# A two-network kernel: where weights are split, where x is scaled, and how the first keys take their turns

## The chip, the cores and the metric

The kernel runs on one core of a Trainium2 chip. The metric is the device time of one execution in microseconds (us). The engines are TensorE (PE in the rows; PEld is its weight load), VectorE (DVE), ScalarE (ACT), GpSimd (POOL) and SyncE (SP), which issues most of the DMAs. Each engine works through its own queue in order; semaphores order the queues among each other.

## The reference, cut to what matters

Two networks run one after the other on x of 512 tokens by 1024 channels. The first has two layers, each an attention mixer and a convolutional gated feed-forward net, and a last norm:

```python
for layer in range(2):
    h = rmsnorm(x, attn_norm[layer])
    x = x + (even_mixer(h, ...) if layer == 0 else odd_mixer(h, ...))
    x = x + conv_glu_ffn(rmsnorm(x, ffn_norm[layer]), ...)
return rmsnorm(x, final_norm)
```

The even mixer holds a stick-breaking attention of 8 heads and a sparse attention of 8 heads; the odd mixer is a forgetting attention of 16 heads. The second network takes that x and a context of 256 tokens:

```python
h  = modulate(rmsnorm_2(x, norm1_g), sh1, sc1);  hc = modulate(rmsnorm_2(ctx, norm1_g), sh1_c, sc1_c)
y_a = neighborhood_attention(q, k, v, k_c, v_c, rpb);  y_b = spatial_gating(gu, gv, ...)
x = x + g1 * merge_branches(y_a, y_b, ga, gb, ...)
x = x + g2 * peer_ffn(modulate(rmsnorm_2(x, norm2_g), sh2, sc2), wq, keys, u, v)
return rmsnorm_2(x, final_g)
```

The first network's last norm scales x itself, since the second network adds to the scaled x. In `peer_ffn` 16 query blocks of 128 columns are scored against 128 keys each, and the 16 best of each are taken.

## The kernel before, in words

**Units.** All weights come in units of 128 output columns by 1024 inputs (some by 1408). SyncE fetches each unit into one of four raw buffers (`fetch_weights`, L182). Products have close to fp32 precision by splitting: ACT rounds the raw unit to `w_hi` (`split_hi`, L201, the copy is L207), and DVE (`split_lo`, L209, L213) or POOL (`split_lo_pool`, L215, L220) makes `w_lo`, what is left. There are two buffers of each, taken in turn, so `split_hi(u)` waits until unit u - 2 has been used. A unit is 24 matmuls of PE on `h_hi` and `h_lo` (`unit`, L222, L239): 16 with `w_hi`, then 8 with `w_lo`. It is a generator that stops after every third matmul, so a block is three matmuls, and `run(steps, n)` issues n blocks. With `ready` it waits for h part by part (eight parts k, one for each 128 channels).

**Norms.** A norm adds squares on POOL, sums them on PE, takes the root on ACT and DVE, spreads it with PE over a bank, and then makes the eight h parts (`shifted_vector`, L408): DVE scales (L413), ACT rounds to `h_hi` (L406), DVE leaves `h_lo` (L416). `norm` (L418) is this for `norm2`, whose h feeds the keys.

**Twin norm.** `twin_norm` (L514) takes the last norm of the first network and the first norm of the second together. While ACT and DVE make the h parts for the neighbourhood attention, POOL scales x in place, two operations for each of eight parts (L576, L578). `ended` and `after` (L278, L282) close a stage: `after(engine, name)` lets an engine wait for all that the named stage has put on PE, DVE, ACT and POOL. The neighbourhood attention (`neighbour`, L1689) begins on ACT, DVE and POOL with such an `after` on the twin norm. There `first_tensor` alternates five blocks of the key unit and five of the value unit, then ends both, then runs the query unit. Sixteen steps follow, four for each of four pairs of heads, with the next pair's units laid between the steps. POOL makes the masks `na_less` of each pair (L1925), three operations each.

**Stacked attentions.** `stick` (stick-breaking, four pairs of heads) and `fox` (forgetting, eight pairs) take four steps for each pair (i = 0 to 3). Pair p + 1's three units (key, query, value) run in blocks between the steps of pair p. What ACT and DVE must do for them is written in two generators, `stacked_scalar` (L1268) and `stacked_vector` (L1281), which the step loop takes up twice in each step with `run(more, 1)`: once behind the first half of the step, once behind the second half. In `stick`, DVE's first half of step m makes `sb_z` and `sb_low` of m (L1454, L1459), and its second half makes the scan and sum of step m - 1 (L1468, L1472). On ACT, the first half ends with Ln and, at i = 0, with the values' copy (L655), and the second half is the exponential of step m - 1 (L1429), which PE turns (L1376) one step later. In `fox` the second half is the exponential (L1600) and the normalisation of step m itself (L671).

**Keys.** `keys` (L2176) runs 16 units on `norm2`'s h. Behind each, ACT copies the query (L2207), PE scores it against the keys (L2194), ACT copies the scores (L2214), and DVE picks the best 16. POOL splits all `w_lo` from the second unit on.

Of the kernel before, what the change touches and what calls it, by code (L numbers as in the profile page):

```python
# [12 lines left out]
ALU = mybir.AluOpType  # L13
# [103 lines left out]
def program(nc, io, table):  # L117
# [38 lines left out]
    def col(name, k=0, n=1):  # L156
        return cols[:, COLS[name] + k:COLS[name] + k + n]
# [258 lines left out]
                ve.scalar_tensor_tensor(lo[:, k - 1, :], hf[(k - 1) % 2][:, 0:n], shift(k - 1), hi[:, k - 1, :], ALU.add, ALU.subtract).then_inc(*dve.next("h", name, k - 1))  # L416

    def norm(name, before, squares, gain, shift):  # L418
        def tensor():
            after(te, before)  # L420
            sums_tensor(name, squares)
            spread_tensor(name, hf[0], t_bank[1])

        def scalar():
            after(sc, before)
            sc.preload_act_table_set("sqrt_and_others")
            root_scalar(name, stat[:, 8:12], stat[:, 4:8])
            for k in range(KT):
                shifted_scalar(name, k, h_hi, T, shift)

        def vector():
            after(ve, before)
            rstd_vector(name)
            ve.wait_ge(*pe.at(name, "spread"))
            shifted_vector(name, x, t_bank[1][:, :], h_hi, h_lo, T, gain, shift)

        tensor()
        scalar()
        vector()
        ended(name)  # L440
# [73 lines left out]
    def twin_norm(name, ctx_name, before, squares, U, hc_blocks):  # L514
# [53 lines left out]
            ve.wait_ge(*pe.at(name, "spread"))  # L568
            shifted_vector(name, x, t_bank[1][:, :], h_hi, h_lo, T, gain, shift)

        def gpsimd():

            gp.wait_ge(*act.at("final", "rstd"))
            for k in range(KT):
                gp.wait_ge(*dve.at(name, "scaled", k))
                gp.tensor_scalar(x[:, k, :], x[:, k, :], col("final_norm", k), None, ALU.mult).then_inc(*pool.next())  # L576
                gp.wait_ge(*pool.here())
                gp.tensor_tensor(x[:, k, :], x[:, k, :], ny[:, :], ALU.mult).then_inc(*pool.next("final x", k))  # L578

        tensor()  # L580
        scalar()
        vector()
        gpsimd()
        ended(ctx_name)

# [678 lines left out]
        return te.matmul(out, q[:, hh, tile], k_lo[:, hh, keys], start=False, stop=True)  # L1266

    def stacked_scalar(U, B, name, p):  # L1268
        yield
        split_hi(U[0] + 1)  # L1270
        yield
        yield
        split_hi(U[1] + 1)
        key_hi(B, name, p)
        yield
        yield
        split_hi(U[2] + 1)
        query_hi(B, name, p)
        yield

    def stacked_vector(U, B, name, p, gain=None, flip=False):  # L1281
        q, k_hi, k_lo, qf, kf, v, vT = B
        yield
        split_lo(U[0] + 1)
        yield
        ve.wait_ge(*w_used.at(U[0]))
        if p:
            ve.wait_ge(*pe.at(name, "v turned", p - 1))
        scaled(kf[:, ::-1] if flip else kf[:, :], lin[U[0] % 2][:, :]).then_inc(*dve.next(name, "k", p))
        bank_of.taken(U[0], dve)  # L1290
        yield
        split_lo(U[1] + 1)
        yield
        key_lo(B, name, p)
        yield
        ve.wait_ge(*w_used.at(U[1]))
        if gain is None:
            scaled(qf[:, :], lin[U[1] % 2][:, :]).then_inc(*dve.next(name, "q", p))
        else:
            ve.scalar_tensor_tensor(qf[:, :], lin[U[1] % 2][:, :], gain, ny[:, :], ALU.mult, ALU.mult).then_inc(*dve.next(name, "q", p))  # L1300
        bank_of.taken(U[1], dve)
        yield
        query_lo(B, name, p)
        yield
        split_lo(U[2] + 1)
        ve.wait_ge(*w_used.at(U[2]))
        scaled(vT[:, ::-1] if flip else vT[:, :], lin[U[2] % 2][:, :]).then_inc(*dve.next(name, "v", p))
# [381 lines left out]
    def neighbour(norm_name, before, st, y_hi, y_lo, U, hc_blocks):  # L1689
# [222 lines left out]
        def gpsimd():  # L1912
            after(gp, before)
            for edge in (slice(0, NA_EDGE), slice(NA_EDGE + T, NA_CTX)):
                for t in (k[0], k[1], vT):
                    gp.memset(t[:, edge], 0.0).then_inc(*pool.next("na edges"))
            for s in range(2):
                gp.memset(less[s][:, 6, :], 0.0).then_inc(*pool.next())
            gp.wait_ge(*mask_in.at("in"))
            for p in range(4):  # L1920
                gp.wait_ge(*bias_in[p % 2].at(p))
                if p >= 2:
                    gp.wait_ge(*dve.at("na least", 1, 4 * (p - 1) - 1))
                for edge in range(3):
                    gp.tensor_tensor(less[p % 2][:, 2 * edge:2 * edge + 2, :], mask[:, edge, :].unsqueeze(1).to_broadcast([P, 2, NA_BAND]), bias[p % 2][:, :, :],  # L1925
                                     ALU.subtract).then_inc(*pool.next("na less", p))
# [249 lines left out]
    def keys(before, st, vals, index, work):  # L2176
# [4 lines left out]
        keys_in = loaded("keys_in")  # L2181

        def tensor():
            for j in range(17):
                if j < 16:
                    run(h_unit(U[j], (lambda k: dve.at("h", before, k)) if j == 0 else None))
                if j:
                    b = (j - 1) % 2
                    te.wait_ge(*act.at("query", j - 1))
# [7 lines left out]
        def scalar():  # L2197
            after(sc, before)
            sc.dma_start(keysT[:, :, :], io["keys"]).then_inc(*keys_in.next("in"))
            for j in range(17):  # L2200
                if j < 16:
                    u = U[j]
                    split_hi(u + 1)
                    sc.wait_ge(*w_used.at(u))
                    if j >= 2:
                        sc.wait_ge(*pe.at("key scores", j - 2))
# [19 lines left out]

        def gpsimd():
            after(gp, before)
            gp.wait_ge(*w_lo_made.at(U[0]))
            for u in U:  # L2230
                split_lo_pool(u + 1)

        tensor()
# [824 lines left out]
```

## Time and profile before

| | us |
|---|---|
| median of 3 runs | 3115.46 (3110.76 to 3118.15) |
| the profiled execution, its own time | 3110.99 |
| its span, first to last instruction | 3109.5 |
| TensorE matmul busy in the span | 2990.8 (96%) |
| VectorE busy | 2261.2 (73%) |
| ScalarE busy | 1337.1 (43%) |
| GpSimd busy | 803.2 (26%) |

The mean granted TensorE clock of the profiled execution is 0.986 of full speed. Busy shares are averages over stages with different limits; times of the stages are read in the trace, in us from the start of the span. In it the stick attention's steps run from 223, those of the forgetting attention from 770, the twin norm's h parts from 1379, the neighbourhood attention's scores from 1420, and the keys from 1799.

### The profile page before, as it was taken

The numbers are of one execution on the slowest core, as the hardware profiler recorded it, in microseconds if no ns is written. First come the engines' busy times: TensorE is split into PE (matmuls) and PEld (weight loads), VectorE is DVE, ScalarE is ACT, GpSimd is POOL, SyncE is SP. The second block draws the span as 40 slices with busy tenths as digits, with TensorE's granted clock in tenths as the row PEclk, the third lists the DMA queues.
The fourth block names the chain that finished last, engine by engine and source line by source line (L and its number), as shares of the span: only waits on it lengthen the run. The fifth ranks groups of instructions, "written<-read, shape, count | busy, mean of one in ns | idle before, by whom it ended". The sixth has DMA issues, their size and how long they took to land. (4 is left out here: it accounts for less than half of the span.)

```text
span 3109.5 us, 43156 instructions
## 1 busy us (share of the span) xinstructions
PE 2990.8 (96%) x16088; PEld 2603.5 (84%) x16088; DVE 2261.2 (73%) x4398; ACT 1337.1 (43%) x2346; POOL 803.2 (26%) x696
## 2 busy tenths in 40 slices
PE   7998899999999999998999989999999999999998
PEld 5666688887777888876778779999999999999998
DVE  4768586775885877743453468978788888988886
ACT  3667532233664323333442234348843333444333
POOL 1000100001001200042000124668744445434431
PEclk9999999999999999999999989999999999999999
DMA  4001244433222444321123223656699999999993
GB/s 149 27 31 49 85 153 143 133 108 105 90 87 96 161 139 132 108 69 57 45 78 102 91 79 111 197 175 231 236 365 330 324 346 337 342 332 321 338 339 117
DMA packets 189710, 525.33 MB, mean 169 GB/s; under 512 B 15792, under 2 KB 80176, under 8 KB 187200
## 3 DMA queue, kind: packets, MB, share of 16 engines
q1 hardware_dynamic: 130432, 308.84, 29.2%
q0 software_dynamic: 45104, 164.68, 14.9%
q10 hardware_dynamic: 13968, 49.06, 4.1%
q8 instruction: 129, 2.11, 0.3%
q14 instruction: 77, 0.63, 0.1%
HBM read 484.22 MB, written 38.31 MB: 168 GB/s over the span
## 5 line engine op out<-in xcount | busy, mean ns | idle before, releaser
L239 PE MATMUL bank<-h_hi,w_hi 128*128 128x512 f32 (+1 forms) x2528 | 958.4, 379 | 44.6 <-DVE h_lo L325 13.1
L239 PE MATMUL bank<-h_lo,w_hi 128*128 128x512 f32 (+1 forms) x2528 | 941.8, 373 | 0.0
L213 DVE TENSOR_TENSOR w_lo<-w_raw,w_hi 128x1024 fp32r<-128x1024 f32 (+1 forms) x452 | 580.2, 1284 | 274.3 <-ACT w_hi L207 255.5
L207 ACT ACTIVATE w_hi<-w_raw 128x1024 fp32r<-128x1024 f32 (+1 forms) x508 | 544.8, 1073 | 458.8 <-PE bank L239 437.4
L239 PE MATMUL bank<-h_hi,w_lo 128*128 128x512 f32 (+1 forms) x2528 | 590.9, 371 | 0.1
L239 PEld LDWEIGHTS bank<-h_hi,w_hi 128*128 128x128 f32 x2528 | 480.2, 190 | 125.7 <-issue 25.6
L239 PEld LDWEIGHTS bank<-h_lo,w_hi 128*128 128x128 f32 x2528 | 481.5, 190 | 58.0 <-issue 2.2
L239 PEld LDWEIGHTS bank<-h_hi,w_lo 128*128 128x128 f32 x2528 | 459.2, 189 | 61.8 <-issue 4.6
L239 PE MATMUL bank<-e_hi,w_hi 128*128 128x384 f32 x1024 | 345.8, 338 | 2.3 <-DVE x L2711 2.0
L239 PE MATMUL bank<-e_lo,w_hi 128*128 128x384 f32 x1024 | 344.5, 336 | 0.0
L2532 POOL DMA_INDIRECT own_row<-in_u_rows,own_e x128 | 166.2, 1298 | 259.7 <-DVE sums L2667 206.6
L2532 POOL DMA_INDIRECT own_row<-in_v_rows,own_e x128 | 176.4, 1378 | 205.5 <-DVE own_row L2661 164.9
L239 PE MATMUL bank<-e_hi,w_lo 128*128 128x384 f32 x1024 | 198.3, 336 | 0.0
L239 PEld LDWEIGHTS bank<-e_hi,w_hi 128*128 128x128 f32 x1024 | 192.5, 188 | 5.8 <-ACT w_hi L207 2.4
L239 PEld LDWEIGHTS bank<-e_lo,w_hi 128*128 128x128 f32 x1024 | 192.7, 188 | 0.0
L239 PEld LDWEIGHTS bank<-e_hi,w_lo 128*128 128x128 f32 x1024 | 179.4, 188 | 0.0
L220 POOL TENSOR_TENSOR w_lo<-w_raw,w_hi 128x1024 fp32r<-128x1024 f32 x56 | 139.2, 2489 | 140.6 <-ACT w_hi L207 140.5
L333 POOL MEMSET sums<- 128x512 f32 x6 | 3.2, 530 | 635.7 <-DVE o_lo L1476 315.2
L2667 DVE SCALAR_TENSOR_TENSOR sums<-own_row,acc_c,sums 128x1024 f32<-128x1024 f32 x127 | 162.5, 1280 | 3.8 <-DVE sums L2667 0.5
L2661 DVE SCALAR_TENSOR_TENSOR own_row<-own_row,own_h 128x1024 f32<-128x1024 f32 x128 | 153.3, 1218 | 0.0
L1054 POOL DMA_DIRECT2D ada_w<-in_ada_w x48 | 25.7, 536 | 467.1 <-DVE ada_w L1073 455.6
L2505 POOL TENSOR_SCALAR oneB<-iota,jT 128x128 f32<-128x128 f32 x192 | 140.5, 748 | 20.2 <-PE bank L2439 16.6
(442 smaller groups left out, 4443.6 us busy)
## 6 DMA issues: line engine op xcount, KB each, us to landing
w_raw<-in_w SPq DMA_DIRECT2D x476, 512.0 KB, 3.9
ada_w<-in_ada_w POOLq DMA_DIRECT2D x48, 512.0 KB, 3.6
expert_weights<-G ACTq DMA_DIRECT2D x12, 2048.0 KB, 7.1
Gin<-expert_weights SPq DMA_DIRECT2D x32, 768.0 KB, 10.1
w_raw<-in_w SPq DMA_DIRECT2D x32, 704.0 KB, 4.0
hidden_ahead<-u_stage ACTq DMA_DIRECT2D x56, 192.0 KB, 3.9
ahead<-hidden_ahead SPq DMA_DIRECT2D x28, 384.0 KB, 8.4
fx_crow<-fox_cum POOLq DMA_DIRECT2D x8, 512.0 KB, 4.0
```

What stands on the lines that cost most here:

```text
L207: sc.activation(w_hi[s][:, 0:n], w_raw[raw_slot[u]][:, 0:n], ACT.Copy).then_inc(*w_hi_made.next(u))
L213: ve.tensor_tensor(w_lo[s][:, 0:n], w_raw[raw_slot[u]][:, 0:n], w_hi[s][:, 0:n], ALU.subtract).then_inc(*w_lo_made.next(u))
L220: gp.tensor_tensor(w_lo[s][:, 0:n], w_raw[raw_slot[u]][:, 0:n], w_hi[s][:, 0:n], ALU.subtract).then_inc(*w_lo_made.next(u))
L239: m = te.matmul(out, wt, moving, start=(not low and k == 0 and moving is hi), stop=(low and k == len(blocks) - 1))
L333: gp.memset(acc[:, :], 0.0).then_inc(*pool.next())
L1054: gp.dma_start(w[r][:, :], io["ada_w"][n]).then_inc(*tile_in[r].next(n))
L2505: gp.tensor_scalar(B[s % HOLD][:, n, :], iota[:, :], jT[:, t:t + 1], None, ALU.is_equal).then_inc(*pool.next("one B", s))
L2532: gp.indirect_dma_start(ring[n % RING][:, :], None, io["u_rows" if kind == "u" else "v_rows"], bass.IndirectOffsetOnAxis(ap=own_e[:, slot: ...
L2661: ve.scalar_tensor_tensor(row, row, 1.0, own_h[:, :, :], ALU.mult, ALU.mult, accum_out=own_a[:, slot:slot + 1]).then_inc(*dve.next("own ro ...
L2667: ve.scalar_tensor_tensor(own_y, row, own_w[:, slot:slot + 1], own_y, ALU.mult, ALU.add).then_inc(*dve.next("own row", n))
```

## The change

- `stacked_scalar` and `stacked_vector`: the split of the pair's second unit stands ahead of the generator's first stop, no longer behind it. This applies to both attentions.
- `norm`: ACT and DVE split the unit behind the next one (the keys' second), ACT ahead of its `after`, DVE behind it and ahead of the root.
- `twin_norm`: POOL's scaling of x is taken out, and `neighbour` calls it on POOL behind the masks of its second pair.
- `keys`: the first two units alternate in five blocks each, both waiting for h part by part. ACT leaves out its first split, and POOL begins with the third unit.

```diff
     def norm(name, before, squares, gain, shift):
+        nxt = taken_units[0]
...
         def scalar():
+            split_hi(nxt + 1)
             after(sc, before)
...
         def vector():
             after(ve, before)
+            split_lo(nxt + 1)
             rstd_vector(name)
...
-        def gpsimd():
-
-            gp.wait_ge(*act.at("final", "rstd"))
-            for k in range(KT):
-                ...
...
-        gpsimd()
         ended(ctx_name)
+
+    def final_x_pool(name):
+
+        gp.wait_ge(*act.at("final", "rstd"))
+        for k in range(KT):
+            gp.wait_ge(*dve.at(name, "scaled", k))
+            gp.tensor_scalar(x[:, k, :], x[:, k, :], col("final_norm", k), None, ALU.mult).then_inc(*pool.next())
+            gp.wait_ge(*pool.here())
+            gp.tensor_tensor(x[:, k, :], x[:, k, :], ny[:, :], ALU.mult).then_inc(*pool.next("final x", k))
...
     def stacked_scalar(U, B, name, p):
+        split_hi(U[0] + 1)
         yield
-        split_hi(U[0] + 1)
         yield
...
         q, k_hi, k_lo, qf, kf, v, vT = B
+        split_lo(U[0] + 1)
         yield
-        split_lo(U[0] + 1)
         yield
...
             for p in range(4):
+                if p == 2:
+                    final_x_pool(norm_name)
                 gp.wait_ge(*bias_in[p % 2].at(p))
...
         def tensor():
+            firsts = [h_unit(u, lambda k: dve.at("h", before, k)) for u in U[:2]]
+            for _ in range(5):
+                run(firsts[0], 1)
+                run(firsts[1], 1)
             for j in range(17):
                 if j < 16:
-                    run(h_unit(U[j], (lambda k: dve.at("h", before, k)) if j == 0 else None))
+                    run(firsts[j] if j < 2 else h_unit(U[j]))
...
-                    split_hi(u + 1)
+                    if j:
+                        split_hi(u + 1)
...
-            gp.wait_ge(*w_lo_made.at(U[0]))
-            for u in U:
+            gp.wait_ge(*w_lo_made.at(U[1]))
+            for u in U[1:]:
                 split_lo_pool(u + 1)
```

## Rows read from the trace of the kernel before

**Rows 1.** Groups by line: shapes, count | busy us, mean ns | idle before, releasers.

```profile
L239 PE MATMUL bank<-h_hi,w_hi 128*128 128x512 f32 (+1 forms) x2528 | 958.4, 379 | 44.6 <-DVE h_lo L325 13.1 <-ACT na_k L1754 10.3 <-DVE h_lo L416 9.1
```

**Rows 2.** Timeline, twin norm into neighbourhood attention: start, length, engine, operation [idle, releaser].

```profile
1381.16 0.75 DVE L416 SCALAR_TENSOR_TENSOR h_lo<-norm_h,mod,h_hi 128x512 fp32r<-128x512 f32 x1 [0.72 <-ACT h_hi L406]
...
1392.36 1.76 DVE L416 SCALAR_TENSOR_TENSOR h_lo<-norm_h,mod,h_hi 128x512 fp32r<-128x512 f32 x1
...
1394.18 0.74 PE L239 MATMUL bank<-h_hi,w_hi 128*128 128x512 f32 x2 [1.16 <-DVE h_lo L416]
...
1397.49 1.98 PE L239 MATMUL bank<-h_hi,w_lo 128*128 128x512 f32 x8
...
1404.35 1.26 POOL L578 TENSOR_TENSOR x<-x,norm_y 128x512 f32<-128x512 f32 x1
...
1408.06 1.06 ACT L207 ACTIVATE w_hi<-w_raw 128x1024 fp32r<-128x1024 f32 x1
...
1409.74 0.76 PE L239 MATMUL bank<-h_hi,w_hi 128*128 128x512 f32 x1 [10.28 <-ACT na_k L1754]
1409.79 5.64 POOL L1925 TENSOR_TENSOR na_less<-na_mask,na_bias 128x512 f32<-128x512 f32 x3 [2.81 <-DMA na_bias<-in_bias]
...
1416.05 1.98 PE L239 MATMUL bank<-h_hi,w_lo 128*128 128x512 f32 x8
1417.87 0.92 PE L651 MATMUL bank<-ident,na_vT 128*128 128x128 f32 x7
...
1419.59 0.71 PE L1817 MATMUL bank<-na_k,na_q 64*128 64x256 f32 x4 [0.80 <-ACT na_v L655]
```

**Rows 3.** Timeline of `norm2` and the first keys.

```profile
1789.32 1.26 POOL L337 TENSOR_TENSOR sums<-sums,norm_h 128x512 f32<-128x512 f32 x1 [4.31 <-ACT norm_h L330]
...
1792.87 0.16 DVE L385 TENSOR_SCALAR stat<-bank 128x4 f32<-128x4 f32 x1 [4.29 <-PE bank L346]
...
1798.49 0.75 DVE L416 SCALAR_TENSOR_TENSOR h_lo<-norm_h,mod,h_hi 128x512 fp32r<-128x512 f32 x1
...
1807.17 1.62 DVE L416 SCALAR_TENSOR_TENSOR h_lo<-norm_h,mod,h_hi 128x512 fp32r<-128x512 f32 x2
...
1808.88 0.33 ACTq L2199 DMA_DIRECT2D keysT<-in_keys  x1
...
1817.81 1.05 PE L2194 MATMUL bank<-keysT,pq 128*128 128x128 f32 x8
```

**Rows 4.** Stretch: length, busy PE, PEld, DVE, ACT, POOL, clock, DMA share, GB/s.

```profile
1440.00:1450.00 10.00, 9.91 (x68) 7.83 (x67) 3.83 (x9) 3.65 (x9) 0.00 (x0) 1.00 0.15 52
```

**Rows 5.** Timeline of the stick attention where pair p = 1 starts.

```profile
249.85 1.22 DVE L1468 TENSOR_TENSOR_SCAN sb_p<-sb_low,sb_soft 128x512 f32<-128x512 f32 x1
...
251.45 0.60 ACT L655 ACTIVATE sb_v<-bank 128x512 f32<-128x512 f32 x1
...
252.80 1.23 ACT L1429 ACTIVATE sb_p<-sb_p 128x512 f32<-128x512 f32 x2 [0.75 <-DVE sb_p L1472]
...
255.00 1.23 DVE L213 TENSOR_TENSOR w_lo<-w_raw,w_hi 128x1024 fp32r<-128x1024 f32 x1 [1.64 <-ACT w_hi L207]
...
255.03 0.50 PE L239 MATMUL bank<-h_hi,w_hi 128*128 128x512 f32 x1 [1.80 <-ACT w_hi L207]
...
256.52 1.03 PE L1376 MATMUL bank<-ident,sb_p 128*128 128x128 f32 x8
256.60 0.75 ACT L1404 ACTIVATE sb_soft<-sb_z 128x256 f32<-128x256 f32 x2 [1.63 <-DVE sb_z L1454]
```

**Rows 6.** Stretches amid the h parts of the twin norm and of `norm2`.

```profile
1388.00:1392.00 4.00, 3.33 (x14) 1.99 (x12) 3.93 (x6) 1.84 (x3) 3.92 (x3) 1.00 0.00 0
...
1806.00:1808.00 2.00, 1.56 (x4) 0.53 (x3) 1.88 (x3) 1.28 (x2) 0.00 (x0) 0.50 0.00 0
```

**Rows 7.** Timeline of the forgetting attention where pair p = 1 starts.

```profile
795.60 0.29 DVE L671 TENSOR_SCALAR fx_p<-fx_p,fx_small 128x128 f32<-128x128 f32 x1
...
800.85 0.38 PE L1551 MATMUL bank<-ident,fx_p 128*128 128x128 f32 x2
```

## What the change does to the time, predicted before it was run

> **What bounds the kernel now.** First the groups of instructions of the whole span, sorted by cost. The reader is to see that TensorE's weight products carry the kernel and that the idle time before them has few releasers: the h parts of two norms, and one ScalarE copy of the neighbourhood attention, `na_k`, alone with 10.3 us [rows 1]. Only work that ends such a wait is worth time here. So I went to the timeline around each wait that the diff touches: the twin norm and the start of the neighbourhood attention, `norm2` and the first keys, and one pair start in each stacked attention.
>
> All sums go by the profiled execution, 3110.99 us with a span of 3109.5 us. It lies 4.47 us under the median of the runs, 3115.46 us, so the same sum is then taken from the median. "PE" is TensorE, "DVE" VectorE, "ACT" ScalarE, "POOL" GpSimd.
>
> **Part 1: x scaling moved off the twin norm.** Two things go.
>
> *Slower h parts.* DVE makes eight h parts from 1381.16 to 1394.12, 12.96 us, and single `h_lo` operations take up to 1.76 us in place of 0.75 [rows 2]. The same eight in `norm2`, with POOL idle, run from 1798.49 to 1808.79, 10.30 us [rows 3]. Without POOL's 16 operations beside them the last part ends at 1381.16 + 10.30 = 1391.46, 2.66 us sooner. From there PE needs what it needs now, 1394.18 to 1399.47, 5.29 us [rows 2], and is free at 1396.8.
>
> The Trainium skill (SBUF — State Buffer, "SBUF: two separate sides") says that the port pair which DVE and GpSimd share is held for a whole instruction, by a DVE operation with two SBUF inputs among others, and the loser blocks fully. By that rule `h_lo` (two SBUF inputs) slows and the scaling by gain (one input in PSUM) doesn't; the trace agrees, and the rule is weighed again below.
>
> *The wait at the neighbourhood attention.* ACT may begin there only when POOL's last scaling is over, at 1405.61; the weights of the query unit are split from 1408.06, and PE starts that unit at 1409.74 after 10.28 us of idleness [rows 2]. Afterwards POOL has nothing queued, so ACT is released by the last h part at 1391.46. The same 2.45 us from release to split give 1393.9; the split must then wait for the key unit, which ends 1.98 us (eight products of the value unit [rows 2]) before 1396.8, so it runs 1394.9 to 1395.9 and the key copy behind it ends at 1396.5. PE is still busy. What is late next is PE itself: the query unit starts at 1396.8, 12.9 us sooner.
>
> *Clock.* That unit's first 16 products take 1409.74 to 1416.05, 6.31 us [rows 2], where the eight behind them, at the full clock, take 1.82 us to the next start at 1417.87, 0.228 each; 16 of these are 3.7 us. PE had been idle for 10 us before. With no idle stretch the 2.6 us go too. Part 1: -12.9 - 2.6 = **-15.5 us**. The bound on the other side: at 1.2 GHz throughout (512 columns are 0.427 us), 48 products from 1382.06 end at 1402.6, a gain of 7.2.
>
> *What could be late in its place.* The masks `na_less`: today they start 4.18 us after the release and take 5.64 [rows 2]; 1391.46 + 9.8 = 1401.3. The first scores come, 15.5 us before 1419.59, at 1404.1. They are covered by 2.8 us.
>
> *Where the scaling goes.* Behind the second pair's masks POOL does the 16 operations, about 25 us as now (the last ends at 1405.61), from about 1411 to 1436. Behind them in its queue are the third pair's masks, wanted some 50 us later, and nobody else. DVE is 3.83 us busy of 10 in that stage while PE is 9.91 busy [rows 4]: slower operations of DVE lie in its idle time. I charge **+0.3**; bounds 0 and +6, for three steps that each show 2 us.
>
> **Part 2: keys' second unit split ahead, first two units interleaved.** *Added:* one `w_hi` split, 1.06 us on ACT [rows 2], and one `w_lo`, 1.23 us on DVE [rows 5], both ahead of `norm2`'s own work. POOL's last square ends at 1790.58 and DVE idles until 1792.87 [rows 3]: the `w_lo` fits into these 2.3 us, and the `w_hi` into ACT's idle time ahead of it. Cost 0; without this cover it would be 1.23. *Moved:* five blocks of three products of each unit alternate, so that when the last h part ends, at 1808.8, 20 products are left in place of 10 + 24.
>
> Whether that pays depends on the clock. Today PE runs two products per h part with gaps, at clock 0.50 [rows 6]. Interleaved, four products of 0.427 us (1.71 us) meet an h part every 1.45 us, so PE has no gap until the clock rises. The twin norm has this pattern already, and there the clock stands at 1.00 in the middle of the h parts, with PE busy 3.33 of 4 us [rows 6]. I take that course: the 20 products need 5.2 us as there, ending at 1814.0. Today key scores begin behind both units at 1817.81 [rows 3]: **-3.8 us**. The other bound: at 1.2 GHz throughout, 48 products from 1799.4 end at 1819.9, +2.1. The keys' table is issued at 1808.88 [rows 3] and has 5.1 us to land. Behind it PE has no gap in the keys, so the gain stays.
>
> The Trainium skill (TensorE: Matmul & The Clock Gate, "What's actually happening") says the clock follows how busy PE has lately been. By that rule the alternation warms it; the row of the twin norm says the same.
>
> **Part 3: second unit's split one stop earlier in the stacked attentions.** This looks like a gain and I read a loss. At the stick attention's pair start PE waits 1.80 us for `w_hi` at 255.03 [rows 5], since ACT puts it behind the exponentials of 252.80 to 254.03. Moved ahead of them it can begin behind the values' copy, at 252.05, and end at 253.1. But `split_lo` moves too: on DVE it now stands ahead of the two scans that start at 249.85, and it must wait for that `w_hi`. Queued behind it are scans, sums and, on ACT, the exponentials. Step by step:
>
> - `w_lo` 253.06 to 254.21; first scan at 254.21 where it was 249.85: +4.36.
> - exponentials 4.36 later: 257.16 to 258.39; PE's turning of the probabilities, now 256.52 [rows 5], at 257.85.
> - ACT's next Abs, now 256.60 [rows 5], behind the exponentials: 258.39, **+1.8**.
>
> PE gets its six products sooner and then waits about 3.1 us in place of 1.8. Both chains are 1.8 late, and PE has no gap behind them to give it back. Pair starts p = 1 and 2 have this form (at p = 0 no scan stands between the stops, at p = 3 no unit is left): **+3.6 us**. Bounds: -3.6, if only PE's wait went; +6.4, if each longer wait drops the clock for 14 products (14 x 0.2 us more).
>
> In the forgetting attention seven pair starts change in the same way: probabilities end at 795.89 and are wanted by PE at 800.85 [rows 7]. They come some 2.3 us later (one w_hi, one w_lo), inside a slack of 4.96: **0**.
>
> **Sum.** -15.5 + 0.3 - 3.8 + 3.6 = -15.4 us. 3110.99 - 15.4 = 3095.6; from the median 3115.46, **3100.1 us**.
>
> **Rivals.**
>
> - *Port conflict where the scaling lands.* By the rule of full blocking every `w_lo` and normalisation of three neighbourhood steps waits for POOL. For: `h_lo` at 1.76 us. Against: DVE 38% busy there. It gives the bound +6: 3105.8. Chance 0.11.
> - *The clock stays low in the interleaved keys.* For: it is 0.50 through today's h parts. Part 2 is +2.1 in place of -3.8: 3106.0. Chance 0.08.
> - *The stacked split does what it says.* DVE has other idle time to take the wait, PE's 1.80 us goes twice: 3100.1 - 7.2 = 3092.9. Against: the scans stand right behind the split. Chance 0.09.
> - *Slower than before.* One mechanism, the DVE queue behind the waiting `split_lo`, in the forgetting attention too: seven starts each expose 1.06 + 1.23 = 2.3 us and 14 products at the low clock (2.7 us), 35 us, beside 6.4 in stick in place of 3.6: 3100.1 + 35 + 2.8 = 3137.9. It decides from the point at which the probabilities come over 4.96 us later. For: stick shows the queue. Against: that slack, and no PE gap in this stretch. Chance 0.04.
> - *The moves do nothing*, since another end, the masks' DMA for one, holds the neighbourhood attention: 3.6 - 3.8 and a third of part 1, 3110. Chance 0.06.
>
> The forecast has the remaining 0.62. A measurement here can tell about 0.2%, 6.2 us, from no change, so faster means under 3109.2. The forecast and the first three rivals lie there, 0.90, less 0.02 for scatter: faster 0.88. Same 0.08, slower 0.04. The range runs from the stick rival to just above the two rivals at 3106, with the runs' scatter: 3092.5 to 3108.5; it leaves out some 0.15.
>
> **What would show it.** Right: no PE idle stretch of 10 us at the start of the neighbourhood attention; `h_lo` in the twin norm at 0.75 us throughout; `na_less` ended before the first scores; the x scaling beside the neighbourhood steps; key scores starting 15 us + 3.8 us sooner, shifted by what stick adds; clock 1.00 from the middle of `norm2`'s h parts. In stick at two pair starts DVE idle for about 3 us before `w_lo` and its scans behind it. In the forgetting attention the same order and no new PE idleness. Wrong: a new releaser of 3 us or more at the start of the neighbourhood attention, waits on `na_pt` in every step, PE waiting on `fx_p`, or a stick stretch that is no longer than before.

## The result, and the profile after

| | us |
|---|---|
| predicted | 3100.1 (3092.5 to 3108.5) |
| changed kernel, median of 5 runs | 3096.45 (3091.01 to 3099.12) |
| kernel before, median of 5 runs beside it | 3113.39 (3109.95 to 3118.15) |
| ratio | 0.9943, 95% interval [0.9928, 0.9958] |
| the profiled execution of the changed kernel: own time, span | 3091.01, 3089.3 |

Faster by 16.9 us between the medians, where 15.4 was forecast; the interval is 13.1 to 22.4 us. The profiled executions are 20.0 us apart (3110.99 - 3091.01): the profiled one after the change is the fastest of its five. What makes executions differ is part of what follows.

All lines behind the first edit are three to ten higher in the changed kernel: L1471 is the scan that was L1468, L1432 the exponential of L1429, L1930 the masks of L1925.

**Groups by line, after** (as [rows 1]). The releaser `na_k` is gone, and the h parts cost 5.8 us in place of 9.1:

```profile
L239 PE MATMUL bank<-h_hi,w_hi 128*128 128x512 f32 (+1 forms) x2528 | 955.3, 378 | 27.8 <-DVE h_lo L325 13.1 <-DVE h_lo L416 5.8 <-ACT w_hi L207 5.4
```

**Timeline, twin norm into neighbourhood attention, after** (answers to [rows 2]):

```profile
1382.21 0.75 DVE L416 SCALAR_TENSOR_TENSOR h_lo<-norm_h,mod,h_hi 128x512 fp32r<-128x512 f32 x1 [0.73 <-ACT h_hi L406]
...
1390.89 1.62 DVE L416 SCALAR_TENSOR_TENSOR h_lo<-norm_h,mod,h_hi 128x512 fp32r<-128x512 f32 x2
...
1396.61 5.76 POOL L1930 TENSOR_TENSOR na_less<-na_mask,na_bias 128x512 f32<-128x512 f32 x3 [2.90 <-DMA na_bias<-in_bias]
1396.86 0.58 ACT L1757 ACTIVATE na_k<-bank 128x512 f32<-128x512 f32 x1
...
1403.15 0.93 PE L654 MATMUL bank<-ident,na_vT 128*128 128x128 f32 x7
...
1404.87 0.71 PE L1820 MATMUL bank<-na_k,na_q 64*128 64x256 f32 x4 [0.79 <-ACT na_v L658]
...
1411.09 2.53 POOL L585 TENSOR_SCALAR x<-x,cols 128x512 f32<-128x512 f32 x1
...
1435.89 1.29 POOL L587 TENSOR_TENSOR x<-x,norm_y 128x512 f32<-128x512 f32 x1
```

Every `h_lo` of the twin norm takes 0.75 us (the line of 1.62 us holds two); the masks end at 1402.4, 2.5 us ahead of the scores; the x scaling runs from 1411.1 to 1437.2. From the first `h_lo` to the first scores it is 22.66 us where it was 38.43: 15.8 us less.

**Waits of PE** from the end of the h parts to the first scores: first the kernel before (1394 to 1420), then after (1392 to 1411). Columns: who waited for what, us in total, times, longest.

```profile
PE bank L239 <- ACT na_k L1754: 10.3, 1, 10.3
PE bank L239 <- DVE h_lo L416: 1.2, 1, 1.2
PE bank L1817 <- ACT na_v L655: 0.8, 1, 0.8
```

```profile
PE bank L1820 <- ACT na_v L658: 0.8, 1, 0.8
```

**`norm2` and the first keys, after** (answers to [rows 3]). DVE's `w_lo` just fits ahead of the root, which follows it without a gap, and the key scores start 6.8 us behind the start of the last two `h_lo`, where it was 10.6 (1807.17 to 1817.81):

```profile
1774.62 1.26 POOL L337 TENSOR_TENSOR sums<-sums,norm_h 128x512 f32<-128x512 f32 x1 [4.31 <-ACT norm_h L330]
...
1776.17 1.23 DVE L213 TENSOR_TENSOR w_lo<-w_raw,w_hi 128x1024 fp32r<-128x1024 f32 x1 [2.29 <-POOL sums L337]
...
1777.31 0.15 DVE L385 TENSOR_SCALAR stat<-bank 128x4 f32<-128x4 f32 x1
...
1791.61 1.62 DVE L416 SCALAR_TENSOR_TENSOR h_lo<-norm_h,mod,h_hi 128x512 fp32r<-128x512 f32 x2
...
1793.31 0.33 ACTq L2208 DMA_DIRECT2D keysT<-in_keys  x1
...
1798.43 1.12 PE L2203 MATMUL bank<-keysT,pq 128*128 128x128 f32 x8
```

**Stretches amid `norm2`'s h parts, after** (as [rows 6]): the clock rises from 0.50 to 1.00 halfway through them.

```profile
1784.00:1786.00 2.00, 1.84 (x4) 1.02 (x5) 1.97 (x4) 0.78 (x2) 0.00 (x0) 0.50 0.00 0
1786.00:1788.00 2.00, 2.00 (x7) 1.56 (x7) 1.97 (x3) 1.28 (x2) 0.00 (x0) 0.65 0.00 0
1788.00:1790.00 2.00, 1.69 (x8) 1.10 (x7) 1.93 (x4) 0.83 (x2) 0.00 (x0) 1.00 0.00 0
```

**Stick attention, start of pair p = 1, after** (answers to [rows 5], everything 0.1 us later by the start of the stage):

```profile
252.03 1.06 ACT L207 ACTIVATE w_hi<-w_raw 128x1024 fp32r<-128x1024 f32 x1
...
253.13 1.22 DVE L213 TENSOR_TENSOR w_lo<-w_raw,w_hi 128x1024 fp32r<-128x1024 f32 x1 [3.09 <-ACT w_hi L207]
254.27 1.22 DVE L1471 TENSOR_TENSOR_SCAN sb_p<-sb_low,sb_soft 128x512 f32<-128x512 f32 x1
...
257.22 1.23 ACT L1432 ACTIVATE sb_p<-sb_p 128x512 f32<-128x512 f32 x2 [4.12 <-DVE sb_p L1475]
...
257.90 1.72 PE L1379 MATMUL bank<-ident,sb_p 128*128 128x128 f32 x8 [3.10 <-ACT sb_p L1432]
258.36 0.71 ACT L1407 ACTIVATE sb_soft<-sb_z 128x256 f32<-128x256 f32 x2
```

This is the order that was worked out, with its times. One thing was not in it: PE's turn of the probabilities takes 1.72 us where it took 1.03 [rows 5], since the clock has fallen behind the 3.10 us wait. **The waits of PE in the whole stick stretch**, before and after, show the exchange: 3.6 us for `w_hi` went, and those for the exponentials rose from 7.2 to 13.2 us.

```profile
PE bank L1376 <- ACT sb_p L1429: 7.2, 8, 2.3
PE bank L239 <- ACT w_hi L207: 3.6, 2, 1.8
```

```profile
PE bank L1379 <- ACT sb_p L1432: 13.2, 8, 3.1
```

### The profile page after: what moved, and what is told of

Same layout as the page of the kernel before. It is cut to its first block and busy times, and to the rows that moved or that the text cites. A ratio compares the mean times of both kernels' runs of the same rounds, so it can differ in the third digit from the quotient of the medians.

```text
span 3089.3 us, 43156 instructions
## 1 busy us (share of the span) xinstructions
PE 2982.5 (97%) x16088; PEld 2599.0 (84%) x16088; DVE 2261.3 (73%) x4399; ACT 1337.1 (43%) x2346; POOL 802.0 (26%) x695
## 5 line engine op out<-in xcount | busy, mean ns | idle before, releaser
L239 PE MATMUL bank<-h_hi,w_hi 128*128 128x512 f32 (+1 forms) x2528 | 955.3, 378 | 27.8 <-DVE h_lo L325 13.1
```

What stands on the lines that cost most here:

```text
L239: m = te.matmul(out, wt, moving, start=(not low and k == 0 and moving is hi), stop=(low and k == len(blocks) - 1))
```

## The experiments

Ten more kernels ran, and the changed one once more. Each is read by four stretches of its trace, which don't depend on when the stage starts: *stick* (first scores to last `o_lo`), *twin* (first `h_lo` to first `na_p`), *neighbour* (first `na_p` to first `merged`) and *keys* (last `h_lo` to first top values). *Landing* is the time from issue to landing of the keys' table. One trace was kept of each run.

| kernel | median us | ratio | stick | twin | neighbour | keys | landing |
|---|---|---|---|---|---|---|---|
| before | 3113.39 | | 116.1 | 39.7 | 207.3 | 11.7 | 4.7 |
| changed | 3096.45 | 0.9943 | 118.6 | 23.9 | 207.3 | 7.9 | 5.0 |
| c1_changed_again | 3094.50 | 0.9941 | 119.2 | 23.9 | 207.2 | 7.9 | 5.0 |
| e7_only_scale | 3099.31 | 0.9950 | 116.1 | 23.9 | 209.9 | 11.5 | 4.6 |
| e8_only_stack | 3116.51 | 1.0008 | 120.4 | 39.5 | 207.2 | 11.6 | 4.8 |
| c2_keys_only | 3111.39 | 0.9992 | 115.3 | 38.8 | 209.9 | 10.3 | 7.3 |
| e1_stack_back | 3093.08 | 0.9934 | 116.2 | 23.9 | 210.0 | 9.3 | 6.3 |
| e2_hi_only | 3091.76 | 0.9932 | 112.1 | 24.0 | 207.2 | 10.7 | 7.1 |
| e4_scale_there | 3102.29 | 0.9964 | 119.3 | 30.2 | 208.8 | 11.2 | 7.3 |
| e6_keys_serial | 3102.02 | 0.9965 | 119.3 | 24.0 | 210.0 | 11.6 | 5.9 |
| e5_no_scale | 3096.31 | 0.9942 | 120.4 | 24.0 | 208.7 | 10.3 | 7.3 |
| f1_keys_table_early | 3094.32 | 0.9937 | 119.0 | 24.0 | 207.2 | 7.8 | 4.8 |
| f2_best | 3090.16 | 0.9925 | 111.8 | 24.0 | 207.2 | 7.9 | 4.9 |

Each ratio is to runs of the kernel before on the same chip, with 95% intervals of about 0.0010 to 0.0017 to either side, which is 3 to 5 us. Between two of these kernels a difference under some 5 us can't be read from the ratios; it is read from the stretches, each of one trace.

### One part alone: the scaling, the stacked splits, the keys

**e7_only_scale** is the kernel before with `final_x_pool` called at `if p == 2:` as in the change, and nothing else.

> The kernel before with one part of the change alone: the scaling of x moved behind the second pair's masks. Theory (the gain of the twin norm belongs to this part alone): the first h_lo of the twin norm to the first na_p of the neighbourhood attention takes 24.0 us in place of 39.7, -15.7 us; h_lo at 0.75 us; the merged outputs begin 207.2 us behind the first na_p as before. The median is 3112.6 - 15.7 = 3097. Stick stretch 116.2 us, last h part to first top values 11.7 us, as before. Rival (part of the 15.7 us comes from the other two parts, or from the clock that they leave): less than 14 us, median over 3099.

Measured: 0.9950 [0.9934, 0.9965], twin stretch 23.9 us. By the ratio, 15.6 us of 3115.09. The whole gain of the twin norm is this part's. Two numbers missed. The median, 3099.31 us, lies just over the rival's 3099, because the kernel before took 3115.09 us beside it and not the 3112.6 from which the expectation was counted. And the neighbour stretch is 209.9 us, not 207.2, with a fallen clock (see below).

**e8_only_stack** is the kernel before with only this, in the scalar generator, and the same for `split_lo` in the vector one:

```diff
     def stacked_scalar(U, B, name, p):
+        split_hi(U[0] + 1)
         yield
-        split_hi(U[0] + 1)
         yield
```

> The kernel before with one part of the change alone: in both stacked attentions the second unit's w_hi and w_lo splits one stop earlier. Theory (the scans and the exponentials queue behind the early w_lo): stick stretch from first scores to last o_lo 118.6 us in place of 116.2, +2.5; forgetting attention 166.9 us as before; median +2.5 over the kernel before, 3115. Rival (the split does what it says and the stick loss in the changed kernel came from elsewhere): the stick stretch is 116 us or less, and the median that of before or up to 7 us under it.

Measured: 1.0008 [0.9998, 1.0017], stick 120.4 us, 4.3 over before, and the forgetting attention's stretch 167.0, as before. A loss by the trace, and larger than the 2.5 us expected; by the ratio alone (+2.5 us) it isn't quite told from nothing.

**c2_keys_only** is the kernel before with the edits in `norm` and `keys` alone.

> The kernel before with one part of the change alone: the second key unit split ahead of norm2 and the first two units interleaved. Theory: last h part to first top values 7.9 us where the keys' table lands in about 5 us and up to 11.2 where it lands in 7, against 11.7 before; the stick attention, the twin norm and the neighbourhood attention as before (116.2; 39.7 from first h_lo to first na_p; 207.2). Median 1 to 4 us under the kernel before. Rival (part of the 3.8 us rests on what the x scaling left behind, so that the part alone gives nothing): 11 us or more from last h part to first top values and the median of before.

Measured: 0.9992 [0.9982, 1.0001], keys stretch 10.3 us: not 7.9, since PE waited 2.19 us for the table, as the expectation allowed for. The reduction belongs to this part alone, but how much of it is kept depends on the table.

**e6_keys_serial** takes the interleaving alone out of the changed kernel; the second unit's split stays ahead:

```diff
-            for _ in range(5):
-                run(firsts[0], 1)
-                run(firsts[1], 1)
```

> The changed kernel with the second unit's split still ahead of norm2's work, but without the alternation: unit one runs by itself with gaps for the h parts, then unit two. Theory (the 3.8 us come from the alternation, half from having 20 in place of 34 products left behind the last h part, half from the clock being up by then): first key scores come 9.0 us behind the last h part as before the change, in place of 5.2, and the granted clock is 0.50 amid norm2's h parts again; the keys are 3.8 us later. Rival (it was POOL's 2.4 us w_lo split that held the second unit): they come within 6.5 us. Rival (the split ahead of norm2 costs time at the sum): the last h part is earlier than in the changed kernel; expected the same within 0.2.

Measured: 0.9965 [0.9952, 0.9977], keys stretch 11.6 us as in the kernel before. The early split is worth nothing without the alternation. By its ratio this kernel is 6.8 us over the changed one; the keys stretch explains 3.7 of that, and the intervals overlap. The expectation gave half of the gain to the number of products and half to the clock. Behind the last h part 34 products are left in the serial order and 20 in the alternating one; an estimate from their 0.228 us at the full clock gives 14 x 0.228 = 3.2 us of the 3.7 to the number, and the small rest to the clock, which stays low up to that point (this is counted, not tested). Two stretches of e6_keys_serial, up to the start of the last `h_lo`:

```profile
1794.00:1796.00 2.00, 1.77 (x4) 0.63 (x3) 1.97 (x4) 0.88 (x2) 0.00 (x0) 0.50 0.00 0
1796.00:1798.00 2.00, 1.55 (x4) 0.53 (x3) 1.88 (x3) 1.28 (x2) 0.00 (x0) 0.50 0.00 0
```

### What the scaling costs, and where

**e4_scale_there** is the changed kernel with the scaling back beside the twin norm's h parts, but ahead of POOL's own `after` in the neighbourhood attention. ACT and DVE no longer wait for it; only POOL's work does:

```diff
         def gpsimd():
+            final_x_pool(norm_name)
             after(gp, before)
...
-                if p == 2:
-                    final_x_pool(norm_name)
```

> The changed kernel with POOL's scaling of x at its old time, beside the twin norm's h parts, but ahead of POOL's own wait for the next stage, so that ScalarE's and VectorE's wait for the twin norm's end does not contain it. It parts the price of the wait from the price of the shared port. Theory: the eight h parts take 12.9 us again in place of 10.3 (single h_lo up to 1.76 us), but ScalarE goes on right behind the last of them, so that PE starts the query unit without the 10.3 us of idleness, about 2.6 us later than in the changed kernel; POOL's edges and masks come 12 us later than there (behind the scaling), masks done at about 15 us behind the last h part, so the first VectorE step waits 2 to 4 us for na_less. First scores of PE 3 to 5 us later than in the changed kernel. Rival (the port conflict is the main price of the old place): h parts slow and most of the 15.8 us is lost again. Rival (the wait alone is the price): h parts at 10.3 us and no loss.

Measured: 0.9964 [0.9952, 0.9977], twin stretch 30.2 us, 6.3 over the changed kernel. Its timeline:

```profile
1387.62 1.47 DVE L416 SCALAR_TENSOR_TENSOR h_lo<-norm_h,mod,h_hi 128x512 fp32r<-128x512 f32 x1
...
1410.41 1.26 POOL L587 TENSOR_TENSOR x<-x,norm_y 128x512 f32<-128x512 f32 x1
...
1412.34 0.95 PE L654 MATMUL bank<-ident,na_vT 128*128 128x128 f32 x7 [2.39 <-POOL na_vT L1920]
1412.66 7.63 POOL L1929 TENSOR_TENSOR na_less<-na_mask,na_bias 128x512 f32<-128x512 f32 x6
...
1414.03 1.23 PE L1820 MATMUL bank<-na_k,na_q 64*128 64x256 f32 x4 [0.74 <-ACT na_v L658]
...
1416.41 0.69 DVE L1900 CUSTOM_DVE_ANT_1 na_p<-bank,na_less 128x512 f32<-128x512 f32 x1 [8.81 <-POOL na_less L1929]
```

The h parts are slow again, and POOL's memsets and masks come late behind the scaling: they are now what PE and DVE wait for. So, taken in this order, the 15.8 us have two parts: the wait of ACT and DVE for the end of the stage, 39.7 - 30.2 = 9.5 us, and then 6.3 us for the place. Of these, 2.7 are the slower h parts (12.99 us from the first to the end of the last, 10.31 in the changed kernel) and 3.6 come with POOL's own work, late behind the scaling, and with a clock that falls behind PE's wait for it (0.50 from 1414 to 1416). In the kernel before that lateness was hidden behind ACT's wait: the masks ended at 1415.4 and the scores came at 1419.6 [rows 2]. Moving the wait alone would have left the second part. The first scores came 5.2 us later than in the changed kernel, where 3 to 5 were expected.

**e5_no_scale** is the changed kernel with the 16 scaling operations left out; x stays unscaled.

> The changed kernel with the scaling of x by norm gain and rstd left out altogether (16 GpSimd operations; x stays unscaled). Theory (beside the neighbourhood steps the scaling costs nothing): first na_p to first merged output is 207.2 or, where the clock falls, 210.0 us, as with it, and the median is the changed kernel's within 1 us. Rival (the shared port or the memory makes the neighbourhood attention wait after all, in the executions with 210.0 us): always 207.2 us or less, no fall of the clock in this stretch, and a median 1 to 3 us lower.

Measured: 3096.31 us, 0.9942 [0.9927, 0.9957], beside 3094.50 and 0.9941 [0.9927, 0.9954] of the changed kernel on the same chip. No cost of the scaling in its new place can be told, though these ratios would not show one under some 5 us. Single operations of DVE do slow down there. The same `w_lo` of the stage, about 13.5 us behind the first `na_p`, first in the changed kernel, then in e5_no_scale:

```profile
1419.67 2.30 DVE L213 TENSOR_TENSOR w_lo<-w_raw,w_hi 128x1024 fp32r<-128x1024 f32 x1
```

```profile
1422.49 1.23 DVE L213 TENSOR_TENSOR w_lo<-w_raw,w_hi 128x1024 fp32r<-128x1024 f32 x1 [0.26 <-ACT w_hi L207]
```

That is 1.1 us more for one operation, and the neighbour stretch is 207.3 us in the changed kernel, as before the change. The cover held. The 208.7 us of e5_no_scale, outside the two values expected, are longer without any scaling; its clock had fallen.

### The stacked attentions

**e1_stack_back** puts both splits of the stacked generators back in the changed kernel; **e2_hi_only** puts back DVE's alone:

```diff
         q, k_hi, k_lo, qf, kf, v, vT = B
-        split_lo(U[0] + 1)
         yield
+        split_lo(U[0] + 1)
         yield
```

> The changed kernel with the stacked attentions' split put back behind the first stop, on ScalarE and VectorE. Theory (VectorE's queue behind the waiting w_lo split costs 1.8 us at each of two pair starts in stick, of which the second is partly paid before already by a fallen clock): the stick stretch, first scores to last o_lo, is 116.1 us as before the change and not 118.6; 1.80 us of PE idleness for w_hi is back at two pair starts; the forgetting attention's stretch (first to last fx_q low part) stays at 166.9; the run is 2.5 us under the changed kernel in the trace. Rival (the 2.5 us came from elsewhere, for example a clock that happened to be lower): the stick stretch stays at 118.6. Rival (the split helps in the forgetting attention): that stretch grows by over 1 us.

> The changed kernel with only ScalarE's split (w_hi) ahead of the first stop; VectorE's split (w_lo) is back behind it, so its scans no longer wait. Theory (the cost is VectorE's queue, the gain is ScalarE's): at the two pair starts of stick the exponentials move by 0.3 us only (ScalarE has the copy ahead of them), PE starts the second unit's products at once, its 1.80 us of idleness goes, and the stick stretch is 112.5 to 114.5 us, under both the kernel before (116.1) and the changed one (118.6); the whole is 4 to 6 us under the changed kernel. Rival (any earlier w_hi delays ScalarE's chain by its own 1.05 us): the stretch is 117 to 118.6. Rival (VectorE and ScalarE bound the pair anyway): 116 us as before.

Measured: e1_stack_back 0.9934 [0.9917, 0.9950], stick 116.2 us, with PE's two waits for `w_hi` back (3.6 us in all); e2_hi_only 0.9932 [0.9915, 0.9948], stick 112.1 us. The forgetting attention's stretch is 166.9 to 167.0 us in both. So the two halves of this edit have opposite signs: ACT's early split alone gives 4.0 us against the kernel before, and DVE's costs 6.5 on top of it. The 112.1 us lie just under the 112.5 to 114.5 expected: 1.7 us are gained at p = 1, and 2.6 at p = 2, where the trace of before has a fallen clock and this one hasn't. The timeline of e2_hi_only at p = 1:

```profile
252.66 1.22 DVE L1471 TENSOR_TENSOR_SCAN sb_p<-sb_low,sb_soft 128x512 f32<-128x512 f32 x1
...
254.75 1.06 ACT L207 ACTIVATE w_hi<-w_raw 128x1024 fp32r<-128x1024 f32 x1
...
255.70 1.15 ACT L1432 ACTIVATE sb_p<-sb_p 128x512 f32<-128x512 f32 x2
256.10 1.22 DVE L213 TENSOR_TENSOR w_lo<-w_raw,w_hi 128x1024 fp32r<-128x1024 f32 x1
257.12 1.02 PEld L1379 LDWEIGHTS bank<-ident,sb_p 128*128 128x128 f32 x8
257.35 1.03 PE L1379 MATMUL bank<-ident,sb_p 128*128 128x128 f32 x8
```

The scans start right behind the sums as before the change. ACT makes `w_hi` while it would wait for them, and the exponentials run without a gap behind it. PE waits neither 1.80 us for `w_hi`, as in [rows 5], nor 3.10 us for the exponentials, as in the changed kernel. Its turn of the probabilities takes 1.03 us, at the full clock, as before the change and not 1.72.

### Why the same kernel takes longer in some executions

**c1_changed_again** is the changed kernel, run once more for a second trace.

> The changed kernel itself once more, for a second trace and more times beside which the others can be read. Theory: two things vary from execution to execution, the landing of the keys' table (4.6 to 7.3 us so far, over 5 us it makes PE wait) and a fall of PE's clock behind the 2.03 us wait for `na_pt` in the neighbourhood attention (first na_p to first merged output 207.2 or 210.0 us). Expected 3094 to 3098 us by the median, stick stretch 118.6, last h part to first top values between 7.9 and 11.2 us. Rival: the stretches repeat within 0.3 us, and the scatter has another source.

Measured: 3094.50 us, 0.9941 [0.9927, 0.9954]; the ratio repeats. The stick stretch is 119.2 us against 118.6, the others repeat within 0.1. This trace has neither a late table nor a fall of the clock in the neighbourhood attention, so it doesn't decide by itself; the table of stretches does. In the kernels that interleave the keys and fetch the table behind the last h part, the keys stretch is 7.9 us where the table lands in 5.0, and 9.3, 10.7, 11.2, 10.3 and 10.3 where it lands in 6.3, 7.1, 7.3, 7.3 and 7.3. PE's rows say it, in c2_keys_only and in e2_hi_only; the third fence is a stretch of e2_hi_only just behind:

```profile
1820.33 1.13 PE L2203 MATMUL bank<-keysT,pq 128*128 128x128 f32 x8 [2.19 <-DMA keysT<-in_keys]
```

```profile
1796.80 1.73 PE L2203 MATMUL bank<-keysT,pq 128*128 128x128 f32 x8 [1.99 <-DMA keysT<-in_keys]
```

```profile
1797.00:1799.00 2.00, 2.00 (x10) 1.90 (x10) 0.00 (x0) 0.43 (x1) 0.00 (x0) 0.54 0.54 178
```

In e2_hi_only the clock stood at 1.00 until the wait and at 0.54 in the stretch behind it. The serial order kept the table out of it: at 5.9 us in e6_keys_serial the stretch is still 11.6.

**f1_keys_table_early** is the changed kernel with the table's DMA issued on ACT's queue at the start of `norm2`, 16.4 us ahead of the last `h_lo`:

```diff
         def scalar():
             split_hi(nxt + 1)
             after(sc, before)
+            sc.dma_start(keysT[:, :, :], io["keys"]).then_inc(*keys_in.next("in"))
...
-            sc.dma_start(keysT[:, :, :], io["keys"]).then_inc(*keys_in.next("in"))
             for j in range(17):
```

> The changed kernel with the keys' table (1 MB, `keysT`) loaded earlier: its DMA is issued on ACT's queue at the start of norm2, some 15 us before the last h part, in place of behind it. Theory: the interleaving of the first two key units shortened the stretch that used to cover this transfer, so that from last h part to first top values an execution takes 7.9 us where the table lands in 5.0 us (profile of the changed kernel) and 10.7 or 11.2 us where it takes over 7. With the early load the table waits in SBUF and the stretch is 7.9 us whatever the landing takes, with no wait of PE for `keysT` and the clock at 1.00. The median then lies 0.5 to 3 us under the changed kernel's, about 3094 to 3096. Rival (the 10.7 and 11.2 us were another effect of the clock, and the table only the name that the profile gave it): the stretch still varies from 7.9 to 11, and the median is the changed kernel's, within 1 us. Second rival: the early transfer delays the weights' transfers or ACT's norm; then norm2's h parts begin later by 1 us or more and the gain is eaten.

Measured: 3094.32 us, 0.9937 [0.9923, 0.9950], keys stretch 7.8 us, no wait for the table. It landed in 4.8 us in this trace, so it would have been in time anyway: the trace shows that the early load costs nothing, not that it saves. By the ratios the difference from 0.9943 and 0.9941 is inside the scatter. That it would save 1.4 to 3.3 us in executions with a late landing stays argued from the other traces; no run shows it.

The second source of scatter is the neighbour stretch, 207.2 to 207.3 us in seven traces and 208.7 to 210.0 in six. In five of the six the clock falls behind a wait of PE for `na_pt`, some 34 us behind the first `na_p`. That wait is 2.03 us in all thirteen traces. (In the sixth, e4_scale_there, it falls earlier, behind the 2.39 us wait that ends at 1412.34.) The wait in the changed kernel and in e7_only_scale:

```profile
PE bank L1837 <- ACT na_pt L658: 2.0, 1, 2.0
```

```profile
PE bank L1833 <- ACT na_pt L654: 2.0, 1, 2.0
```

Stretches behind that wait, of e7_only_scale, then of the changed kernel:

```profile
1442.00:1444.00 2.00, 2.00 (x17) 1.64 (x13) 1.29 (x4) 0.89 (x3) 0.00 (x0) 0.55 0.00 0
1444.00:1446.00 2.00, 1.42 (x8) 0.90 (x8) 0.00 (x0) 0.85 (x2) 0.00 (x0) 0.50 0.25 63
```

```profile
1440.00:1442.00 2.00, 1.74 (x23) 1.33 (x19) 1.30 (x4) 1.53 (x6) 0.00 (x0) 1.00 0.00 0
1442.00:1444.00 2.00, 1.52 (x10) 1.12 (x11) 0.27 (x1) 0.43 (x2) 0.00 (x0) 1.00 0.33 125
```

It isn't the moved scaling: c2_keys_only has 209.9 us with the scaling in its old place, and e5_no_scale 208.7 with none. What decides in which executions it falls stays open. The Trainium skill (TensorE: Matmul & The Clock Gate, "What's actually happening") says that the chip judges PE's activity in a rhythm of its own, which doesn't restart with the kernel. That would fit the same waits with two outcomes; no run here can show it.

### The version that the experiments point to

**f2_best** joins e2_hi_only's edit and the early table.

> The changed kernel with two edits: VectorE's `w_lo` in the stacked attentions back behind the scans (ScalarE's `w_hi` stays ahead), and the keys' table loaded at the start of norm2. Theory: both gains are independent. The stick stretch from first scores to last o_lo takes 112.1 us in place of 118.6 (-6.5), the keys' stretch from last h part to first top values 7.9 us. By medians: the run with the w_lo edit alone gave 3091.8, and the table another -1 to -2: 3089 to 3091. Rival (the table's landing doesn't matter for the median): 3091.8 within 1 us.

Measured: 3090.16 us (3082.34 to 3092.91), 0.9925 [0.9912, 0.9939]; stick 111.8 us, keys 7.9 us. It has the lowest median of all kernels here, 23 us under before by its ratio. Its waits of PE in the stick stretch:

```profile
PE bank L1380 <- ACT sb_p L1433: 8.2, 8, 2.3
PE bank L1350 <- ACT sb_pt L1419: 2.5, 3, 1.8
```

The `w_hi` wait is gone, and the exponentials' wait is near its old 7.2. Against the changed kernel the gain rests on the stick stretch, -6.8 us, seen in both traces that have this edit; the ratios' intervals overlap.

## Why the prediction was right, point by point

**Part 1, h parts and wait: -12.9, -2.6 for the clock, +0.3 for contention.** Measured 15.8 us from first `h_lo` to first scores and to first `na_p`, where 15.5 was charged. The parts of it stand too: no `h_lo` over 0.75 us, no idle stretch at the query unit, and the first of its products at the full clock. The masks' slack was put at 2.8 us and is 2.5. The contention was real in single operations and 0.0 us in the stretch, not 0.3.

The Trainium skill (SBUF — State Buffer, "SBUF: two separate sides") was weighed in the prediction: a DVE operation with two SBUF inputs and a GpSimd operation that reads SBUF block each other. The trace agrees in kind, `w_lo` at 2.30 us beside the scaling and 1.23 without it. The prediction priced full blocking in that stage at up to +6 us; none was paid, and DVE had idle time around these operations [rows 4].

**Part 2, keys: -3.8.** Measured 11.7 to 7.9 us, just this, where the table lands in 5.0 us. That is 0.1 us less than the "5.1 us to land" which the prediction took as enough, from one transfer in one trace (4.7 us): the full gain in the profiled execution is in part luck. In five of the seven traces where the interleaved keys fetch it late, it lands in 6.3 to 7.3 us, and 1.4 to 3.3 us of the 3.8 are given back. This step was mis-sized in what it left out, and so the part is probably worth less in the median: the ratio of c2_keys_only gives 2.5 us, but its interval, -0.3 to 5.6, holds 3.8 too.

**Part 3, stacked splits: +3.6 in stick, 0 in the forgetting attention.** In the two profiled executions the stick stretch grows by 2.5 us. Over all traces it is 118.6 to 120.4 us with both splits early (seven traces, mean 119.5) and 115.3 to 116.2 without (four, mean 115.9): +3.6, the number forecast. The mechanism is right, but that the mean meets the number is in part luck, because the prediction had the clock at 1.00 for both pair starts, and it wasn't. From the first scores of p = 1 to those of p = 2, 29.2 us in all four traces without the edit, it is 30.8 us in the two with it in which the clock stays up: +1.6, where 1.8 was worked out. It is 30.9 to 31.0 and 32.1 us in the five in which PE's longer wait takes the clock down. From p = 2 to p = 3 the profiled pair shows only +0.76, because in that execution of before the 1.80 us wait had already taken the clock down; in c2_keys_only, with the same code there and no such fall, this step is 30.0 us and not 30.8. The last pair, which the edit does not touch, adds up to 0.6 us in six of the seven, with one more fall of the clock. Before the change, at p = 2:

```profile
287.39 1.74 PE L1376 MATMUL bank<-ident,sb_p 128*128 128x128 f32 x8
```

against 1.03 us at p = 1 [rows 5]. In the forgetting attention the stretch is 166.9 us before and after. The probabilities end at 800.11 and are wanted at 803.37: 3.3 us of the 4.96 us of slack in [rows 7] are left, so they came 1.7 us later where 2.3 was worked out.

**The rivals.** The port conflict cost nothing that these runs can tell (e5_no_scale, and the neighbour stretch of 207.3 us before and after). The low clock in the interleaved keys didn't come: it was 1.00 from halfway. The stacked split does not do what it says, as written; but the rival's case, both waits of PE gone, is what ACT's half alone does (e2_hi_only: -4.0 us). The prediction treated the two splits as one edit and so missed that one half of it was worth keeping. The slower case needed more than 4.96 us of delay in the forgetting attention, and it was 1.7. The masks' DMA released POOL at 1396.61 and was covered.

**The total.** The parts alone give ratios of 0.9950, 1.0008 and 0.9992, together 0.9950, or -15.6 us; the whole gave 0.9943 and 0.9941, -17.7 and -18.4. These agree within their intervals. In the profiled pair, of the 20.2 us by which the spans differ, 15.8 + 3.8 - 2.5 = 17.1 are these three parts. The rest is clock and luck of the pair, which the sum did not hold. 1.6 us are the stretch between the last `a_in` and the twin norm's first `h_lo`, 82.4 before and 80.8 after, which no edit touches. There the granted clock is 0.50 from 1371 to 1377 before, and after it is 1.00 from 1371 to 1374 and 0.56 from 1374 to 1377. The stretch is 80.5 to 80.9 in ten traces, e8_only_stack and c2_keys_only with the old twin norm among them, and 82.4 in three. These three (before, e7_only_scale, e1_stack_back) all have the old stacked splits, and so has c2_keys_only with its 80.5; whether the earlier stage has a hand in it is not shown. 0.9 us more are between the last `merged` and `norm2`'s last h part (64.4 and 63.5; 64.3 or 64.4 in six of the other eleven traces), again with PE's products there at the lower clock, and the remaining 0.6 are small differences elsewhere.

## What to carry to other kernels

Work that nobody needs soon should not stand in the stage whose end others wait for: taking it out of that wait and out of the way of its own engine's next tasks are two gains, here 9.5 and 6.3 us, the second with 2.7 us of slower h parts in it. When an early preparation is spread over two engines, decide for each engine by what is queued behind it: an engine that would only idle there takes it for nothing, and one that must wait for the other delays all behind it. When a stretch gets shorter, look again at each transfer that it used to cover, and with more than one measured landing.

## What the runs showed of the hardware that was not expected

- One DMA of 1 MB, issued at the same point of all but two of these kernels, landed in 4.6 to 7.3 us over thirteen traces: at most 5.0 in seven of them, two with early issue, and 5.9 and more in six.
- With the same waits of PE, the granted clock stayed at 1.00 in some executions and fell to 0.50 in others, at one place of the neighbourhood attention (five of thirteen traces); these traces are 1.5 to 2.8 us longer there, and one profile can't tell it.
- GpSimd and VectorE slow each other where one runs 128x512 products and the other `w_lo` (1.23 to 2.30 us; the first product of the scaling took 2.53 us), and a whole stage can carry this without being longer (207.3 us before and after).
